# A chunked recurrence's first two phases, done PSUM bank by PSUM bank

## The reference, cut to what matters

```python
def step(s, inp):
    r_t, w_t, k_t, v_t, a_t, b_t = inp
    sa = jnp.einsum('bhvk,bhk->bhv', s, a_t)
    s = s * w_t[:, :, None, :] + sa[..., None] * b_t[:, :, None, :] + v_t[..., None] * k_t[:, :, None, :]
    return s, jnp.einsum('bhvk,bhk->bhv', s, r_t)
```

## Time and profile before

| | us |
|---|---|
| median of 3 runs | 3112.61 |
| lowest and highest | 3110.99, 3114.48 |
| the profiled execution, its own time | 3113.62 |
| its span in the profile | 3111.5 |
| TensorE busy in the span | 2906.1 (93%) |
| VectorE busy | 2107.1 (68%) |
| ScalarE busy | 1291.6 (42%) |

### The profile page before, as it was taken

One profiled execution on the slowest core, in us unless ns is written; L12 is line 12 of the kernel. 1 busy time (PEld: TensorE's weight loads), 2 busy tenths in 40 slices (PEclk: granted clock), 3 DMA queues, 4 the chain that ended last, 5 costly groups with the idle time before them and its releaser, 6 DMA issues. The chain is left out here.

```text
span 3111.5 us, 69988 instructions
## 1 busy us (share of the span) xinstructions
PE 2906.1 (93%) x27683; PEld 2361.1 (76%) x27683; DVE 2107.1 (68%) x3303; ACT 1291.6 (42%) x2293; POOL 685.4 (22%) x681
## 2 busy tenths in 40 slices
PE   8999999978898998999799999989989999998898
PEld 7899999967777776778698878877756666667676
DVE  9526666647667555887477787615649888886676
ACT  1225555524344434443311111111238888875432
POOL 5000000002232220111021111100027666664111
PEclk9999999989899998999899999999999999999999
DMA  6624545454353446664579999955450201008441
GB/s 208 215 86 145 154 151 153 152 162 128 90 123 86 119 132 180 177 179 120 207 260 337 355 354 340 330 181 184 148 188 1 69 32 38 15 22 255 137 163 71
DMA packets 461470, 501.90 MB, mean 161 GB/s; under 512 B 199105, under 2 KB 348850, under 8 KB 456122
## 3 DMA queue, kind: packets, MB, share of 16 engines
q1 hardware_dynamic: 373466, 339.83, 35.9%
q10 hardware_dynamic: 79168, 141.59, 12.9%
q0 software_dynamic: 8512, 16.02, 1.7%
HBM read 357.13 MB, written 140.39 MB: 160 GB/s over the span
## 5 line engine op out<-in xcount | busy, mean ns | idle before, releaser
L3101 POOL TENSOR_TENSOR sp_att<-sp_beta,sp_left 128x512 f32<-128x512 f32 (+3 forms) x320 | 302.3, 955 | 434.3 <-DVE sp_left L3062 419.9
L120 PE MATMUL po_acc<-po_x_high,po_w_low 128*128 128x412 f32 (+1 forms) x840 | 301.1, 359 | 13.5 <-DVE po_x_low L113 12.9
L120 PE MATMUL pe_acc<-pe_x_high,pe_w_low 128*128 128x412 f32 (+1 forms) x840 | 302.9, 361 | 5.3 <-PEq L86 5.3
L121 PE MATMUL po_acc<-po_x_low,po_w_high 128*128 128x412 f32 (+1 forms) x840 | 294.6, 351 | 0.0
L122 PE MATMUL po_acc<-po_x_high,po_w_high 128*128 128x412 f32 (+1 forms) x840 | 294.2, 350 | 0.0
L121 PE MATMUL pe_acc<-pe_x_low,pe_w_high 128*128 128x412 f32 (+1 forms) x840 | 293.9, 350 | 0.0
L122 PE MATMUL pe_acc<-pe_x_high,pe_w_high 128*128 128x412 f32 (+1 forms) x840 | 293.6, 350 | 0.0
L3062 DVE TENSOR_TENSOR_SCAN sp_left<-sp_z,sp_left,sp_zero 128x512 f32<-128x512 f32 x192 | 235.7, 1269 | 18.5 <-ACT sp_z L3023 14.2
L2722 DVE TENSOR_TENSOR po_work<-po_work,po_q 128x1024 f32<-128x1024 f32 x128 | 173.7, 1357 | 77.1 <-DMA po_work<-in_cache_k 69.6
L3015 ACT ACTIVATE sp_beta<-sp_z,sp_bias 128x512 f32<-128x512 f32 (+3 forms) x320 | 183.2, 629 | 91.4 <-PE sp_z L2950 45.7
L1353 ACT COPY po_o<-po_acc 128x412 f32<-128x412 f32 (+1 forms) x105 | 52.4, 502 | 382.8 <-PE po_acc L122 347.5
(11 more groups left out here) (491 smaller groups left out, 6962.8 us busy)
## 6 DMA issues: line engine op xcount, KB each, us to landing
po_work<-in_cache_k SPq DMA_DIRECT2D x256, 256.0 KB, 4.9
po_work<-in_cache_v ACTq DMA_DIRECT2D x256, 256.0 KB, 4.7
scratch_ops<-pe_work SPq DMA_DIRECT2D x160, 128.0 KB, 2.0
out_z<-pe_o SPq DMA_DIRECT2D x84, 206.0 KB, 2.8
pe_w<-in_w_e SPq DMA_DIRECT2D x21, 512.0 KB, 5.9
out_z<-po_o ACTq DMA_DIRECT2D x17, 616.0 KB
rc_opx<-scratch_ops SPq DMA_DIRECT2D x64, 160.0 KB, 3.7
po_w<-in_w_o ACTq DMA_DIRECT2D x20, 512.0 KB, 5.9
```

The source lines that it names most:

```text
L120: pe.matmul(out, ll, rh, start=start, stop=False)
L121: pe.matmul(out, lh, rl, start=False, stop=False)
L3101: pool.tensor_tensor(att[h][:, n % 3, 0:w], be[h][:, n % 4, 0:w], left[h][tile(n) % 2][:, at + 1:at + 1 + w], ALU.mult).then_inc(at_ok[h], 1)
```

## The change

VectorE's three products of M_ are each split into one per bank (six instructions, bank 0's three first), and TensorE's KV phase is split likewise: for bank 0 it waits for the first three products, does the two transposes and then the four matmuls of that bank (r = 0), and then the same for bank 1 (r = 1). The counts of the semaphores `x0` and `m_sb` double.

```diff
                 elif ph == KV:
                     if c == 0:
                         pe.wait_ge(cst, 96)
-                    pe.wait_ge(x0, c + 1)
-                    pe.wait_ge(m_sb, c + 1)
                     if c == 0:
                         pe.wait_ge(kv_in, 16)
-                    for g, r, s in tiles:
-                        pe.matmul(b[half[s], r, wide(g)], op(K_T, r, s, g), o[half[r], A_T:R_T + 1, 2 * g + s, :],
-                                  start=True, stop=True)
-                    for k, n in ((2, V_), (3, K_T)):
-                        for g in (0, 1):
-                            mm = pe.transpose(b[:, g, turned(k)], pair(o[:, n, 2 * g:2 * g + 2, :]), idt[:, :])
+                    for x in (0, 1):
+                        pe.wait_ge(x0, 2 * c + x + 1)
+                        pe.wait_ge(m_sb, 2 * c + x + 1)
+                        for k, n in ((2, V_), (3, K_T)):
+                            pe.transpose(b[:, x, turned(k)], pair(o[:, n, 2 * x:2 * x + 2, :]), idt[:, :])
+                        for g, r, s in tiles:
+                            if r == x:
+                                mm = pe.matmul(b[half[s], r, wide(g)], op(K_T, r, s, g),
+                                               o[half[r], A_T:R_T + 1, 2 * g + s, :], start=True, stop=True)
                     mm.then_inc(k_pe, 1)
...
                 if ph == M_:
                     dve.wait_ge(m_pe, c + 1)
-                    dve.tensor_tensor(by_bank(xx[q][:, :, :, :]), grouped(b[:, :, 4 * CH:6 * CH]), spread(lev0[:, :]),
-                                      ALU.mult).then_inc(x0, 1)
-                    dve.tensor_tensor(lv[q][:, LV_O:LV_M + 1].rearrange("p n s g c -> p s g n c"),
-                                      b[:, :, 0:4 * CH].rearrange("p s (g n c) -> p s g n c", g=2, n=2),
-                                      every(outer[:, :], 2).rearrange("p s (g n c) -> p s g n c", g=2, n=2), ALU.mult)
-                    dve.tensor_tensor(rt[q][:, :, :, :], b[:, :, 0:4 * CH].rearrange(
-                        "p s (g n c) -> p s g n c", g=2, n=2)[:, :, :, 0, :], spread(inner[:, :]), ALU.mult).then_inc(m_sb, 1)
-                    dve.wait_ge(x0, c + 1)
+                    for x in (0, 1):
+                        products = b[:, x, 0:4 * CH].rearrange("p (g n c) -> p g n c", g=2, n=2)
+                        dve.tensor_tensor(by_bank(xx[q][:, :, :, :])[:, x], grouped(b[:, :, 4 * CH:6 * CH])[:, x],
+                                          spread(lev0[:, :])[:, x], ALU.mult).then_inc(x0, 1)
+                        dve.tensor_tensor(lv[q][:, LV_O:LV_M + 1].rearrange("p n s g c -> p s g n c")[:, x], products,
+                                          outer[:, :].rearrange("p (g n c) -> p g n c", g=2, n=2), ALU.mult)
+                        dve.tensor_tensor(rt[q][:, x], products[:, :, 0, :], spread(inner[:, :])[:, x],
+                                          ALU.mult).then_inc(m_sb, 1)
+                    dve.wait_ge(x0, 2 * c + 2)
```

## The result

The changed kernel is slower. Its median over 20 runs is 3123.3 us (3117.29 to 3131.52), that of the kernel before over its 20 runs 3112.24 us; the ratio is 1.0035 with a 95% interval of 1.0025 to 1.0045, that is 8 to 14 us. The forecast was 3124.2 us. A second set of 11 runs beside 29 of before gave 1.0026 (1.0012 to 1.0040).

A forecast was written before the change was run, and what follows sets the result against it. TensorE was taken as the bound, wholly so in the S5 chunks. Costs of 7.5 (S5 chunks), 1.0 (ten full-clock chunks) and 3.1 us (six half-clock chunks) made 11.6, so 3112.6 + 11.6 = 3124.2 us; range 3109 to 3136.

The forecast's parts named there:

- S5 chunks: 16 chunks with S5 work after M_, bound by TensorE: 0.47 us slower each, 7.5 us in all.
- Quadrants: KV's matmuls: a bank's tiles use two quadrants, so eight rounds instead of four, +0.43 us.
- The change-over into KV that falls away: Between S5's whole-array matmuls and KV, which now begins with transposes: 0.11 us saved, up to 0.20.
- Chunks that wait, full clock: Ten chunks without S5 work after M_: longer KV offsets earlier release, 0.1 us slower each, 1.0 us in all.
- Chunks at the half clock: Six chunks: KV 1.04 us longer, release 0.53 us earlier, so 0.51 us slower each, 3.1 us in all.
- The line that I had drawn: Test of the forecast: wrong if the granted clock after 745 us leaves 0.84 by more than 0.05.
- The uncovered 7.4 us: VectorE's extra 0.23 us in each of 32 chunks if no other wait covered it; costed at nothing.
- The wait before KV: TensorE's stand until VectorE has read the banks: to fall from 13.3 us to about 3.
- a bank's tiles run one after the other: Rival in KV: sixteen rounds per bank pair, +0.85 us in each of 32 chunks, 3151 us; chance 0.08.
- the far end of it with loads in the open: Rival's extreme in KV: weight loads not hidden either, another 55 us, 3206 us; chance 0.01 of the 0.08.
- The clock: Rival: clock stays up between 745 and 830 us, 3108.8 us, no change that can be told; chance 0.12.
- four tiles take two rounds: Rival in KV: a bank needs two rounds, not four, so the earlier release pays: -4.8, 3107.8 us; chance 0.07.

The follow-up runs named there:

- the one with the eight matmuls together: Changed kernel with its waits and transposes per bank kept, but KV's eight matmuls in all four quadrants between the transpose pairs: ratio 1.0000, 3115.30 us.
- TensorE's half alone: Kernel before with only TensorE's KV split by bank, VectorE's products unsplit: ratio 1.0035, 3127.26 us against 3114.29.
- VectorE's half alone: Kernel before with only VectorE's products split into six; TensorE's KV waits for both banks: ratio 1.0011, 3116.71 us against 3114.29.
- with the quadrants kept: Changed kernel with each bank's transposes behind its wait, but all eight KV matmuls behind both, in four quadrants: ratio 0.9985, 3111.99 us.
- the version with three phases turned: Kernel before with transposes ahead of matmuls in KV, N1 and N2, nothing split: ratio 0.9966, 3105.67 us against 3115.12.

## Why the prediction was right

**The sign and the size.** 11.6 us were forecast; 10.9 (8 to 14) were measured. The likeliest case came out, not a rival. The mechanism and its cost in the S5 chunks are shown. That the whole sum came within 1 us is in part luck: the other two terms were off, one up and one down.

**Quadrants.** +0.43 us for eight rounds in place of four, from LINK's 1.09 against 0.67 us. Measured 0.41 us, as the difference in the chunk time between the changed kernel and the one with the eight matmuls together. This was the step that carried the forecast, and it held although LINK's two quadrants share neither rows nor columns and KV's share their rows.

**S5 chunks.** 0.47 us each was forecast and 0.41 came (0.46 in the four chunks 2 to 5, whose S5 work is the table products). The term that was a little off is the transposes: behind S5's whole-array matmuls the first two take 0.31 us until the matmuls (914.63 to 914.94), not 0.37. The change-over into KV that falls away was 0.09 us (1.06 us from line 1979 to KV before, 0.97 now), where I took 0.11. Together 4 x 0.46 + 12 x 0.41 = 6.8 us, where I had 7.5. The prediction's three windows miss one of the 16 chunks: chunk 12 has its KV at 847.95, ahead of 850. The S5 stretches (chunks 12 to 18 and 26 to 31) grew by 1.9 to 2.5 us, where about 3 was forecast for each window.

**Chunks that wait, full clock.** +0.05 us was worked out for this one chunk, +0.01 came, with KV's start 0.53 us earlier as forecast and the second wait holding nothing. The kernel with TensorE's half alone shows what the early release hides, 0.52 us. But the 0.1 us that I charged on average does not hold over the stage: the eight chunks from 18 to 26 together are 4.2 us longer in the first profile and 1.6 in the second. Beside it stand the stalls before XT and in LINK, 4.1 and 3.5 us, for which the prediction had no term.

**Chunks at the half clock.** Here the mechanism was right and the count was not. The wait fell from 1.21 to 0.68 us as worked out, and a chunk that is wholly at the half clock costs 0.46 us more, where 0.51 was forecast. But the sum took six such chunks from one profile, and from 745 to 830 us the two profiles of the changed kernel have a granted clock of 0.89 and 0.90 in place of 0.84. The line that I had drawn (wrong if it leaves 0.84 by more than 0.05) was reached by the first and passed by the second. Chunks 6 and 8, at the half clock before, run KV at the full clock in both. Which chunks meet a half-clock stretch differs between profiles of kernels whose TensorE program is the same: of the three chunks that start KV from 781 to 815 us, all at the half clock before, two run it at the full clock in the kernel with VectorE's half alone, where the window's clock is 0.98. So 3.1 us for this term has no run behind it: from chunk 6 to 12 the stage is 1.1 and 0.9 us shorter in the two profiles, not longer. The some 4 us that the measured time has beyond the S5 chunks are not split up further by the timed runs.

**VectorE.** 0.23 us more per chunk, costed at nothing: it was 0.20, and its half alone gave 0.9999 to 1.0024. The uncovered 7.4 us that I had called no likely bound are at the edge of that interval; the stage, 487.6 against 489.9 us, shows none of it.

**The wait before KV.** About 3 us was forecast to be left, 5.9 was. The difference is chunk 0: it waited 3.8 of the 13.3 us before and waits 2.9 of the 5.9 now. So 0.89 us for each of 15 chunks was no good mean; the other 14 waited 0.68 us each.

**The rivals.** That a bank's tiles run one after the other is refuted: eight instructions take four rounds (0.58 us with the change-over), not eight. So is the far end of it with loads in the open. The clock was somewhat higher from 745 to 830 us, but never stayed up, and the kernel is slower all the same. Over whole executions it did not move: the mean granted clock is 0.9747 in the 11 timed runs of the changed kernel and 0.9749 in the 29 of before beside them. With levels of 2.4 and 1.2 GHz that difference is worth at most 0.6 us (0.0002 of 3115), so the clock is not the cost. That four tiles take two rounds is refuted by the same 0.58 us.

**Not foreseen.** N1_'s first matmuls start beside the last ones of KV. I had counted a phase as done before the next one starts. It made no difference here: from bank 1's first matmul to N1_'s transposes it is 1.05 us (915.89 to 916.94), which is four rounds, 0.43, and the 0.62 that N1_'s matmuls took before (916.90 to 917.52). The stalls from chunk 18 to 26 were not foreseen either.

## What to carry to other kernels

Before splitting a phase by bank to release it earlier, look at which quadrants of TensorE's array the pieces use: here all tiles of a bank lay in one half of the rows, and half the work took as long as all of it. In this kernel a change between matmuls in quadrants and whole-array transposes cost 0.1 to 0.17 us, so it is worth trying to put a phase's transposes next to other whole-array work; in three phases that gave 7 to 14 us. An early release is worth at most what can run before the second piece is released: with the quadrants kept that was two transposes, 0.22 us, and VectorE's split took as much back. And read such a gain over all chunks, not in one: here the chunks with the early release were not shorter in sum.

## What the runs showed of the hardware that was not expected

- TensorE does not keep the order of issue between quadrants, so "nothing is reordered at run time", as I described the kernel, does not hold for the starts of its matmuls. In the changed kernel N1_'s line 2300 starts at 915.92 while six of bank 1's instructions (line 2246) are still to start, and eight matmuls issued row by row take 0.68 us in place of 0.67. Whole-array instructions between them do keep them apart: 0.58 us for bank 0's half alone.
- Less TensorE busy time did not give its whole time back: in the version with three phases turned TensorE is busy for 22.4 us less and the kernel is about 10.6 us faster. Beside it stand half-clock stretches and stalls, of up to 1.4 us before line 2367 in the S5 chunks 12 to 17, that the profile can only call issue. In the whole stage these stalls come to 7 us in the profile of the kernel before, the fewest of all, to 17 in this version, and to 13 and 14 in the kernels with VectorE's half alone and with the order of issue changed:

```profile
PE rc_bk L2367 <- issue: 1.4, 1, 1.4
```

- Two sets of runs of one kernel, 12 and 11 of them, gave 0.9992 to 1.0013 and 0.9969 to 0.9986, each beside the kernel before on its own chip, at the same mean granted clock of 0.975.
